# A two-block model on one NeuronCore: the norms, the value turning and the forget gate of the second attention dealt into its weight blocks, and another order of tiles

## The reference, cut to what matters

```python
def shared_kv(h, w_kv, f_bias, k_gain):
    k, v, fl = jnp.split(h @ w_kv, [B_W, 2 * B_W], axis=-1)
    k = rms_norm(k.reshape(B, T, B_HEADS, HEAD_DIM), k_gain)
    v = v.reshape(B, T, B_HEADS, HEAD_DIM)
    log_f = jax.nn.log_sigmoid(fl.astype(jnp.float32) + f_bias.astype(jnp.float32))
    c = jnp.cumsum(log_f, axis=1).transpose(0, 2, 1)
    return k, v, c

def fox_attention(h, w_q, q_gain, w_out, k, v, c):
    q = rms_norm((h @ w_q).reshape(B, T, B_HEADS, HEAD_DIM), q_gain)
    ...
        s = jnp.einsum('bqhd,bshd->bhqs', q[:, q0:q1], k[:, :q1],
                       preferred_element_type=jnp.float32) * scale
        decay = c[:, :, q0:q1, None] - c[:, :, None, :q1]
        s = jnp.where(causal, s + decay, -jnp.inf)
        p = jax.nn.softmax(s, axis=-1).astype(v.dtype)
        outs.append(jnp.einsum('bhqs,bshd->bqhd', p, v[:, :q1]))
    ...
    return o.reshape(B, T, B_W) @ w_out
```

## Time and profile before

| | us |
|---|---|
| median of 3 runs | 3098.51 |
| lowest and highest | 3095.84, 3099.16 |
| the profiled execution | 3099.07 |
| its span in the trace | 3097.3 |

### The profile page before, as it was taken

How to read it: one execution, slowest core, us unless ns; L and a number is a source line. 1 busy time by engine, 2 the same in 40 slices (tenths; PEclk the granted TensorE clock), 3 DMA queues, 4 the chain that set the end, 5 groups by cost and what they waited for, 6 DMA issues and landing times.

```text
span 3097.3 us, 51399 instructions
## 1 busy us (share of the span) xinstructions
PE 2912.5 (94%) x19181; PEld 2556.3 (83%) x19181; DVE 1470.5 (47%) x2251; ACT 1050.5 (34%) x1793; POOL 1166.9 (38%) x652
## 2 busy tenths in 40 slices
PE   6988999998999999999989899999999879999998
PEld 6967989986898777888778789999999748878776
DVE  2664555554330365242678655444361234464333
ACT  4752223222324333222424464222232235522222
POOL 3413444431444444444445303444444400144443
PEclk8988999999999999999999899999999889999999
DMA  2210000001222222222211001222222100122222
GB/s 101 88 48 1 1 1 1 2 1 42 93 90 89 95 93 92 95 95 95 101 63 46 24 1 62 87 90 89 88 86 91 68 1 1 35 89 95 95 89 94
DMA packets 56858, 194.97 MB, mean 63 GB/s; under 512 B 7872, under 2 KB 8234, under 8 KB 56724
## 3 DMA queue, kind: packets, MB, share of 16 engines
q1 hardware_dynamic: 52960, 189.36, 17.4%
q10 hardware_dynamic: 3764, 3.74, 0.4%
HBM read 190.98 MB, written 2.10 MB: 62 GB/s over the span
## 4 chain that ended last, share of the span: by engine, by line
issue 43%; PE 16%; POOL 11%; DVE 4%; ACT 1%; DVEq 1%; POOLq 0%; ACTq 0%; PEldq 0%; PEld 0%
POOL wl L445 11%; PE ps L479 8%; PE ps L2020 2%; PE ps L2051 2%; DVE work L1927 1%; PE ps L2038 1%; DVE top L1924 1%; PE ps L854 1%; PE ps L842 1%; PE ps L1643 1%; POOLq L128 0%; PE ps L1884 0%; DVE hinv L880 0%; PE ps L2023 0%; DVEq L1925 0%
## 5 line engine op out<-in xcount | busy, mean ns | idle before, releaser
L445 POOL TENSOR_TENSOR wl<-wraw,wh 128x1024 fp32r<-128x1024 f32 x353 | 875.0, 2479 | 1261.4 <-ACT wh L437 1261.3
L437 ACT ACTIVATE wh<-wraw 128x1024 fp32r<-128x1024 f32 x353 | 372.5, 1055 | 563.9 <-PE ps L479 476.1
L479 PE MATMUL ps<-xah,wh 128*128 128x264 f32 (+1 forms) x2672 | 498.0, 327 | 25.2 <-ACT xah L808 14.2
L479 PE MATMUL ps<-xah,wl 128*128 128x264 f32 (+1 forms) x2672 | 488.3, 323 | 0.0
L479 PE MATMUL ps<-xal,wh 128*128 128x264 f32 (+1 forms) x2672 | 486.8, 322 | 0.0
L479 PEld LDWEIGHTS ps<-xah,wh 128*128 128x128 f32 x2672 | 405.4, 189 | 75.7 <-issue 19.6
L479 PEld LDWEIGHTS ps<-xah,wl 128*128 128x128 f32 x2672 | 404.0, 189 | 41.3 <-issue 0.8
L479 PEld LDWEIGHTS ps<-xal,wh 128*128 128x128 f32 x2672 | 402.5, 188 | 40.7
L627 DVE TENSOR_TENSOR res<-res,stage 128x512 f32 (+3 forms) x112 | 81.8, 730 | 440.2 <-ACT stage L543 440.2
L479 PE MATMUL ps<-xbh,wh 128*128 128x264 f32 (+1 forms) x1392 | 273.1, 336 | 13.4 <-POOL wl L445 12.8
L479 PE MATMUL ps<-xbl,wh 128*128 128x264 f32 (+1 forms) x1392 | 269.5, 333 | 0.0
(11 more groups left out here) (307 smaller groups left out, 3620.5 us busy)
## 6 DMA issues: line engine op xcount, KB each, us to landing
wraw<-in_w SPq DMA_DIRECT2D x353, 512.0 KB, 3.2
res<-in_x SPq DMA_DIRECT2D x4, 528.0 KB, 5.8
res<-in_x ACTq DMA_DIRECT2D x1, 2048.0 KB, 7.9
out<-res SPq DMA_DIRECT2D x1, 2048.0 KB, 7.1
masks<-in_masks ACTq DMA_DIRECT2D x1, 614.5 KB
cossin<-in_cossin ACTq DMA_DIRECT2D x1, 528.0 KB
tri<-in_tri ACTq DMA_DIRECT2D x1, 87.8 KB
ident<-in_ident ACTq DMA_DIRECT2D x1, 64.0 KB
```

The lines of the kernel that those rows point to most:

```text
L437: act.activation(wh[:, s * DM:(s + 1) * DM], wraw[:, s * DM:(s + 1) * DM], ACT.Copy).then_inc(hi_done, 1)
L445: pool.tensor_tensor(wl[:, s * DM:(s + 1) * DM], wraw[:, s * DM:(s + 1) * DM], wh[:, s * DM:(s + 1) * DM].bitcast(F32), ALU.subtract).then ...
L479: mm = pe.matmul(ps[:, 2 * s + h, 0:width], ws[:, s * DM + kk * P:s * DM + (kk + 1) * P], x[:, at:at + width], start=(h not in [o[0] for o ...
```

## The change

The three segments `foxkv`, `foxf` and `foxq` become one of 25 blocks, `fox`, with the order of weights: forget gate, 8 k, 8 q, 8 v. The barriers around the stage behind them go. Its work is written into the engines' lists block by block: `pe_fox` has the sums of k and q squares behind blocks 2 to 17, the k spreads in the middle of and behind blocks 11 to 14, the q spreads in the middle of and behind blocks 19 to 22, and the value turns behind blocks 18 to 24, the last one behind the first three scores of the attention. `act_fox` splits the weights, squares, takes the roots, copies v without scaling to `stage` and stores the turned values scaled by a turned `rstd` (`fox_tok`). `dve_fox` runs the forget gate as a generator, one piece in each of eight blocks, then inverses and multiplications. `pool_fox` writes `headrow` behind the splits of blocks 9 to 12. `qz`, `headrow`, `decay_row`, `lfneg` and `cneg` move in SBUF, so that they can be written while `xah` and `xal` are read. `ORDER` becomes (0, 1, 2, 3, 4), for both attentions, with other banks for the transposes. In the first attention's stage GpSimd's zeroing of `qz` no longer waits for the last products.

```diff
-ORDER = (4, 0, 3, 1, 2)
+ORDER = (0, 1, 2, 3, 4)
...
-    add("foxkv", 16)
-    add("foxf", 1)
-    add("foxq", 8)
+    add("fox", 25)
...
+            if midway is not None and i == len(order) // 2:
+                midway(pe)
...
-        pool.wait_ge(block_done, b0 + 10)
         zero_halves(pool)
...
-    TURN_BANK = {4: 4, 0: 6, 3: 4, 1: 5, 2: 6}
-    TURN_BACK = {4: 2, 0: 2, 3: 2, 1: 3, 2: 3}
+    TURN_BANK = {0: 4, 1: 5, 2: 6, 3: 4, 4: 5}
+    TURN_BACK = {0: 2, 1: 2, 2: 3, 3: 3, 4: 2}
...
+    def pool_fox(pool):
+        for j in range(25):
+            split_lo(pool, Blk(FOX + j + 1, 0))
+            if j == 9:
+                pool.drain()
+                pool.memset(headrow[:, :, :], 0.0)
+            if 10 <= j <= 12:
+                pool.drain()
+                rows = slice(32 * (j - 10), 32 * (j - 10) + 16)
+                pool.tensor_copy(headrow[rows, :, :], ident[0:16, 0:HEADS].unsqueeze(2).broadcast_to([16, HEADS, C]))
+            pool.drain()
...
+        if fox:
+            pe.wait_ge(acc_free, SEGS["fox_out"].b0)
         for n in range(3):
             scores(n)
+        if begun is not None:
+            begun(pe)
...
+        dve.wait_ge(block_done, SEGS["fox_out" if fox else "dsa_out"].b0)
         dve.memset(rowsum[:, :, :], 1.0)
...
+    def pe_fox(pe):
+
+        def sums(n):
+            m = n % 8
+            pe.wait_ge(f_sq, n + 1)
+            if n == 8:
+                pe.wait_ge(f_root, 1)
+            for h in range(2):
+                mm = pe.matmul(ps[0:16, 4 + h, 0:HT], win64[:, 14 - 2 * m:30 - 2 * m],
+                               fox_sq[n % 2][:, h * HT:(h + 1) * HT], start=(m == 0), stop=(m == 7))
+            mm.then_inc(f_used, 1)
+
+        def spreads(n):
+            m = n % 8
+            pe.wait_ge(f_inv, n // 8 + 1)
+            wait(pe, f_app, n)
+            for h in range(2):
+                mm = pe.matmul(ps[:, 6 + h, 0:HT], fox_spread[:, m * P:(m + 1) * P], fox_inv[:, h * HT:(h + 1) * HT],
+                               start=True, stop=True)
+            mm.then_inc(f_spread, 1)
+
+        for j in range(25):
+            x = (xbh, xbl) if 9 <= j <= 16 else (xah, xal)
+            first = dict(fresh=4, sums=pe_sums()) if j == 0 else dict(fresh=5) if j == 9 else {}
+            n = 2 * (j - 11) if 11 <= j <= 14 else 8 + 2 * (j - 19) if 19 <= j <= 22 else None
+            if n is not None:
+                first["midway"] = lambda pe: spreads(n)
+            products(pe, Blk(FOX + j, 0), *x, KT, **first)
+            if j == 1:
+                pe.wait_ge(acc_free, FOX + 1)
+                for c in range(NCH):
+                    mm = pe.matmul(ps[0:ROWS[c], 7, c:c + 1], rstd[0:1, c * C:ENDS[c]], ones[0:1, 0:1],
+                                   start=True, stop=True)
+                mm.then_inc(f_turn, 1)
+            if 2 <= j <= 17:
+                sums(j - 2)
+            if n is not None:
+                spreads(n + 1)
+            if j >= 18:
+                fox_values(pe, j - 18)
+
+    def fox_values(pe, m):
+        pe.wait_ge(acc_free, FOX + 18 + m)
+        if m == 0:
+            pe.wait_ge(f_root, 2)
+        wait(pe, f_vout, m)
+        for c in range(NCH):
+            mm = pe.transpose(ps[0:ROWS[c], 4 + c // 4, (c % 4) * P:(c % 4 + 1) * P],
+                              stage[:, m % 2 * T + c * C:m % 2 * T + ENDS[c]], ident[:, :])
+        mm.then_inc(f_vturn, 1)
...
+        for j in range(25):
+            split_hi(act, Blk(FOX + j + 1, 0))
+            if j == 0:
+                root(act)
+            if j < 8:
+                split_residual(act, j, 6, xbh, False)
+            if j == 2:
+                act.wait_ge(f_turn, 1)
+                act.activation(fox_tok[:, 0:4], ps[0:C, 7, 0:4], ACT.Copy)
+                act.activation(fox_tok[0:ROWS[4], 4:5], ps[0:ROWS[4], 7, 4:5], ACT.Copy)
+                act.wait_ge(sp_abs, 2)
+                act.activation(fox_sp[0][:, :], lfneg[:, :], ACT.Abs)
+                act.drain()
+                act.activation(fox_sp[1][:, :], fox_sp[0][:, :], ACT.Exp, scale=-1.0).then_inc(sp_exp, 1)
+            if 2 <= j <= 17:
+                if j == 10:
+                    roots(0)
+                square(j - 2)
+            if j == 18:
+                roots(1)
+            if j >= 18:
+                raw(j - 18)
+            if j >= 19:
+                store(j - 19)
+        raw(7)
+        store(6)
+        store(7)
...
+        for j in range(17):
+            b = Blk(FOX + j, 0)
+            if j == 0:
+                root(dve)
+            dve.drain()
+            dve.wait_ge(block_done, num(b) + 1)
+            dve.wait_ge(acc_free, num(b))
+            if j == 0:
+                dve.tensor_tensor(two(lfneg[:, :]), acc(b, 16), two(rstd[0:16, :]), ALU.mult).then_inc(acc_free, 1)
+                dve.drain()
+            else:
+                x = tile_at(pf, j - 1 if j < 9 else j + 7)
+                dve.tensor_tensor(two(x), acc(b), two(rstd[:, :]), ALU.mult).then_inc(acc_free, 1)
+            if j < 8:
+                low(dve, j)
+                next(forget)
...
+            if j == 9:
+                inverse(0)
+            if j == 10:
+                apply(0)
+            if 11 <= j <= 14:
+                apply(2 * (j - 11) + 1)
+                if j < 14:
+                    apply(2 * (j - 11) + 2)
+        inverse(1)
+        for n in range(8, 16):
+            apply(n)
```

More of the change, by code:

```diff
@@ L1859, in dve_dsa @@
                           ALU.mult)
[L1861 to L1888, removed]
     IX = 2 * (NCH - 1)
@@ L2153, in dve_attention @@
         store(HEADS // 2 - 1)
-    def dve_fox(dve):
-        def tile_post(t0):
-            def post(j, u, b):
-                dve.tensor_tensor(two(tile_at(pf, j + t0)), acc(b), two(rstd[:, :]), ALU.mult).then_inc(acc_free, 1)
-            return post
-        def forget_post(j, u, b):
-            dve.tensor_tensor(two(lfneg[:, :]), acc(b, 16), two(rstd[0:16, :]), ALU.mult).then_inc(acc_free, 1)
-        dve_scaled(dve, "foxkv", tile_post(0), dve_root(), lows(5, 6, xbh, xbl))
-        dve_scaled(dve, "foxf", forget_post)
-        dve_scaled(dve, "foxq", tile_post(16))
+    FOX = SEGS["fox"].b0
@@ new lines, in fox_values, with act_fox, square, roots @@
+    def fox_values(pe, m):
[7 more added lines that the diff above has]
+        mm.then_inc(f_vturn, 1)
+    def act_fox(act):
+        root = act_root()
+        def square(n):
+            m = n % 8
+            act.wait_ge(acc_free, FOX + n + 2)
+            wait(act, f_used, n - 1)
+            act.activation(fox_sq[n % 2][:, :], tile_at(pf, m if n < 8 else 16 + m), ACT.Square).then_inc(f_sq, 1)
+        def roots(i):
+            act.wait_ge(f_used, 8 * (i + 1))
+            act.activation(two(fox_root[:, :]), pair_of(4, 16), ACT.Sqrt, bias=eps[0:16, 0:1], scale=1.0 / 64
+                           ).then_inc(f_root, 1)
+        def raw(m):
+            b = Blk(FOX + 17 + m, 0)
+            act.wait_ge(block_done, num(b) + 1)
+            act.wait_ge(acc_free, num(b))
+            act.activation(two(stage_at(m % 2)), acc(b), ACT.Copy).then_inc(acc_free, 1)
+        def store(m):
+            act.wait_ge(f_vturn, m + 1)
+            for c in range(NCH):
+                last = act.activation(vtok[0:ROWS[c], c, m * P:(m + 1) * P],
+                                      ps[0:ROWS[c], 4 + c // 4, (c % 4) * P:(c % 4 + 1) * P], ACT.Copy,
+                                      scale=fox_tok[0:ROWS[c], c:c + 1])
+            last.then_inc(f_vout, 1)
+        for j in range(25):
[25 more added lines that the diff above has]
+        store(7)
@@ L2169, in dve_forget @@
     def dve_forget(dve):
+        one, e, r, p, q = (t[:, :] for t in fox_sp)
         dve.tensor_scalar(lfneg[:, :], lfneg[:, :], rowvec[:, 2:3], -1.0, ALU.add, ALU.mult)
+        dve.drain().then_inc(sp_abs, 1)
+        yield
+        yield
+        dve.wait_ge(sp_exp, 2)
+        dve.tensor_scalar(r, e, 2.0, None, ALU.add)
+        dve.memset(one, 1.0)
+        yield
         dve.drain()
-        dve_softplus(dve, cneg[:, :], lfneg[:, :])
-        dve.memset(sp[0][:, :], 1.0)
+        dve.reciprocal(p, r)
```

121 lines of the change are left out of this document (67 added, 54 removed).

## The result

| | us |
|---|---|
| before, median of 4 runs | 3097.47 (3095.84 to 3099.16) |
| after, median of 4 runs | 3062.77 (3062.36 to 3063.94) |
| ratio, 95% interval | 0.9889 [0.9877, 0.9900] |
| after, the profiled execution | 3062.58, span 3060.8 |

The change is 34.7 us faster, where 54.3 was forecast; 3062.77 lies just above the range. The two spans, cut at the same places, show which terms missed. The cuts are starts of TensorE's rows, except that the end of the old blocks is the recorded end of their last product, with its tail; by that measure the new blocks end 0.17 us later than the 2498.04 used here.

What follows compares the result with a forecast made beforehand. TensorE, busy 94% of the span, was taken to bound the kernel. Last product to last turned output -84.0, added in the blocks +33.7, first attention -4.0: -54.3 us from 3098.5, forecast 3044, range 3034 to 3062.

Steps and rivals of the forecast that it cites:

- The hole: Stage between fox's last product and the second attention's first scores: 78.9 us with two barriers, all removed.
- the work dealt out: Fox blocks: the other engines' moved work hides under TensorE's blocks of 5.84 us, 6.7 with a pair of inserts.
- From the last product to the first values: Second attention's new start: first values 8.0 us after the last product, including a new wait of about 2.3.
- the order of tiles: Both attentions: ascending order removes two waits in each head, gaining 5.7 us in the second and 4.0 in the first.
- rival A: Both attentions: new order gains nothing or adds equal ScalarE waiting at tile 2; 3054, or 3063; chance 0.16.
- The pair of sums: Inserts in the fox blocks: two float32 matmuls cost 0.88 us a pair, 0 to 0.1 besides for their surroundings.
- The wait for tile 2's copy in the first attention: ScalarE's copy comes late there: a wait of 0.3 us in half of the heads.
- The first attention's start: Small tiles first: no gain in the forecast sum, another 1 to 3 us only as a possibility under rival D.
- rival D: No extra insert cost and better overlap at attention's start, or first attention's start gains 1 to 3: 3036; chance 0.12.
- The clock at the second attention's start: Assumed to stay high over the new TensorE wait of about 2.3 us; no cost counted.
- Rival B: Fox blocks: Vector Engine held by GpSimd's split delays posts and squares; 12 to 24 us, 3056 to 3068; chance 0.14.
- Rival C: Fox blocks: ScalarE's in-order turn becomes the period, slower than before; 3123 with turns of 10 us; chance 0.03.

Runs made afterwards that it cites:

- e7: The changed kernel without the forget gate's reciprocal and logarithm series, so another function is computed; 3064.44 us, ratio 0.9888.
- e3: The changed kernel with the turned output of a pair issued two units later in both attentions; 3047.44 us, ratio 0.9840.
- e6: e3 with ScalarE copying tile 2's turned probabilities ahead of tile 4's exponential in both attentions; 3038.16 us, ratio 0.9801.
- e2: The kernel before with only the ascending order of tiles and its banks; 3100.0 us, ratio 1.0008.
- e11: The changed kernel with one more unused reciprocal of 3.44 us on the Vector Engine in each of turns 3 to 7; 3072.28 us, ratio 0.9918.
- e8: The changed kernel with a tiny exponential between the stores of values 6 and 7, loading the table ahead; 3061.91 us, ratio 0.9879.
- e9: e3 with squares summed by a 128 x 128 matrix, no spreads, roots and reciprocals tile by tile, forget gate whole under the value blocks; 3026.99 us.
- e10: e9 with the edit of e6 added; 3016.36 us, ratio 0.9737.

## Why the prediction was wrong, point by point

**The mechanism that carries the gain was right.** The hole and its barriers are gone, TensorE stays busy in every block, and the work dealt out is hidden: for the forget gate's series e7 shows it, for the rest the blocks without a wait. From the last product to the first values were 8.5 us, forecast 8.0.

**The step that failed is the order of tiles.** The prediction worked out which waits the new order removes in a plain head, and it removes them. It then took that pace for all heads, without following the ring of banks through a head that also turns an output. There the new order puts the output's two banks ahead of tile 0 and sends its scores to a bank of tile 4. The price is 0.99 x 7 = 6.9 us of start distance in the second attention, where the whole miss is 7.4. The start's 0.5 makes up the rest only because two other terms nearly cancel: the low clock behind the first values cost 1.4, and the heads without the wait were 1.8 faster in all than forecast (a pair takes 16.05 in e3, not 16.30). In the first attention a pair without either wait takes 15.49 us (e6). After's 17.72 is that, 1.32 for the bank (1.78 between the starts of output and scores, less 0.46) and 0.75 for tile 2's copy, with 0.16 left over, most of it in the matmuls right behind the waits (0.08 and 0.05). The forecast was 16.74 - 0.54 = 16.20: it had 0.3 for the copy and nothing for the bank. So the forecast gain of 5.7 + 4.0 was, with the order alone (e2), 3.2 less 2.9, and those 3.2 came from the start and not from the heads.

This is rival A by its result, but not by its reason. A was priced at 3054, and at 3063 with 0.3 us more in each head; that the second price was met is luck. A named ScalarE's late copy at tile 2; that wait is there in the first attention only, and it is still there in e3, which is 15.3 us faster.

**Terms mis-sized.** The pair of sums: taken as 0.88 from the start distance of dsa_b's rotations, L1661 in the earlier trace rows, which have 128 weight columns as the products have; measured 1.17 with 16, and that is the 3.9 missed in the blocks. The wait for tile 2's copy in the first attention: 0.3 in half of the heads, measured 0.75 in as many (in the others the bank wait covers it; in e3, where that is gone, they lose 0.37). The first attention's start: not counted, while first values come 5.3 us after the first scores instead of 9.1, a gain of 3.8 us, which rival D had at 1 to 3. Not all of it is the small tiles: in e3 and e6 the same start took 6.8, at a mean clock of 0.54 and not 0.70, so about 2.3 are the tiles and 1.5 the clock. The slower start of dsa_out, 1.5, was not counted, and it too goes with the clock: in e11, whose first attention is that of after, the start took 6.5 and dsa_out began at 1.00. The clock at the second attention's start: assumed high, was 0.72, which cost 0.2 before the first values and 1.4 behind them.

**Rival B** has its mechanism shown and its price refuted for this change: 0 here, and 7 to 9 only with 17 us more on the Vector Engine. By the Trainium skill (SBUF — State Buffer, "Who interferes with whom") a Vector Engine instruction with two SBUF inputs and a GpSimd instruction that reads SBUF exclude each other; the trace agrees, with 2.72 us beside the split and 0.69 behind it. **Rival C** shows nowhere: ScalarE is busy 38.6 of 130 us in the blocks.

**The range.** A and the small misses were treated as alternatives, with 0.55 left for a forecast that needed all of them absent. They came together. By the table the first attention missed by 6.9 (7 pairs at 1.52 each are 10.6, less the 3.8 of the start), the way to fox by 1.5, the blocks by 3.9, the stretch behind them by 7.4, and all that is left gave back 1.9. That is 17.8 of 54.3. Taken from the profiled execution of before, 3099.1 - 54.3 + 17.8 = 3062.6, which is what after's took. The heads of the two attentions are most of it.

## What to carry to other kernels

When an order of work changes, write out the ring of buffers over one full period, the rare members too (here the output of every second head), and ask of each bank who read it last and when; a plan that is right for the common head can lose its whole gain in the rare one. Price an insert between matmuls from a row with the same number of weight columns, and from the distance of starts, also behind it. Before dealing work into an engine's gaps add it up turn by turn with the longer durations that stand beside GpSimd's work: here 6.6 of 7.1 us in the fullest turn just fitted. And before a gain or a loss at a start is put down to the change, look at the granted clock there in several runs: here it differed between runs with the same instructions.

## What was not expected of the hardware

Two float32 matmuls of 264 columns between products with 128 weight columns cost 0.89 us with 128 weight columns and 1.17 with 16; fewer columns were slower. Beside GpSimd's split an instruction with one SBUF input (TENSOR_SCALAR) and a running sum with two were also held until it ended; the Vector Engine of after:

```profile
2334.61 2.62 DVE L2262 TENSOR_SCALAR fox_sp<-fox_sp 16x528 f32<-16x528 f32 x1
...
2369.85 3.27 DVE L2286 TENSOR_TENSOR_SCAN lfneg<-fox_sp,cneg 16x528 f32<-16x528 f32 x1
```

In e11, where the scan began before the split, it lasted 1.25; a TENSOR_SCALAR of that size lasts 0.42 elsewhere in after. A reciprocal that started beside the split kept its 3.44. And one wait of 2.30 us on TensorE, at the same place among the same instructions, had a mean clock of 0.72 around it in four profiled executions and 1.00 in two. With waits of 1.08 (e8) and 0.88 (e9, e10) it was 1.00.
